# Hybrid Mamba-2 and dilated-attention layer: group 0's B and C beside the samples' values, and one norm matmul a group

## The reference

```python
u = _rmsnorm(x, norm_w) @ w_in                       # 1024 -> z, x|B|C, dt, q, k, v, z_att, gates
xbc = silu(causal_conv(xbc, conv_state, conv_w) + conv_b)
xs, Bm, Cm = split(xbc)                              # B and C: one 128-wide vector per group, 4 groups
dt = softplus(dt_raw + dt_bias);  A = -exp(a_log)
y = ssd_chunked(xs, dt, A, Bm, Cm, ssm_state) + d_skip * xs
yg = (y * silu(z)) per group of 512 channels
yg = yg * rsqrt(mean(yg * yg over the group) + EPS)  # the grouped norm
br_ssd = (yg * ssd_norm_w) @ w_ssd_br
# attention: three head groups, (window, dilation) = (128,1), (512,4), (2048,16)
o = sum over g of alpha_g * o_g,  alpha = softmax of the groups' log sums
br_att = (o * silu(z_att)) @ w_att_br
out = x + (sigmoid(g_ssd) * br_ssd + sigmoid(g_att) * br_att) @ w_out
```

## Time and profile before

| | us |
|---|---|
| median of 3 runs | 1121.01 |
| lowest, highest | 1118.74, 1121.52 |
| the profiled execution's own time | 1128.53 |
| its span | 1126.7 |
| mean granted clock of PE | 0.962 of full speed |
| PE busy | 1032.8 (92% of the span) |
| DVE, ACT, POOL busy | 701.6, 534.6, 242.0 |

### The profile page before, as it was taken

The page is one execution under the profiler, slowest core; times in us unless marked ns, Lnnn a source line. Parts: engine busy times, 40 slices in busy tenths (PEclk is TensorE's granted clock), DMA queues, the critical chain, the costliest instruction groups (busy, mean ns, idle before and its releaser), DMA issues.

```text
span 1126.7 us, 21757 instructions
## 1 busy us (share of the span) xinstructions
PE 1032.8 (92%) x8474; PEld 953.1 (85%) x8474; DVE 701.6 (62%) x1113; ACT 534.6 (47%) x1273; POOL 242.0 (21%) x327
## 2 busy tenths in 40 slices
PE   3999898898989897999999999999998999599998
PEld 2999788888888875359998998998998999599998
DVE  6867574656566357545887887887853576933432
ACT  5335556455555645115546456556443775511210
POOL 0312121222222100001211212112200988300000
PEclk9999999999999998768999999999998999799999
DMA  9543443254511245542533561571496997332221
GB/s 366 225 178 114 156 192 130 83 236 143 232 60 56 83 161 208 161 176 113 229 136 150 230 247 41 227 284 61 173 351 262 338 348 313 121 118 111 75 104 48
DMA packets 30310, 198.28 MB, mean 176 GB/s; under 512 B 4536, under 2 KB 6808, under 8 KB 20704
## 3 DMA queue, kind: packets, MB, share of 16 engines
q1 hardware_dynamic: 25712, 183.35, 42.8%
q0 software_dynamic: 4496, 13.54, 3.1%
HBM read 180.16 MB, written 104.70 MB: 253 GB/s over the span
## 4 chain that ended last, share of the span: by engine, by line
PE 58%; DVE 18%; ACT 13%; issue 7%; DMA 3%; SPq 0%; POOL 0%; DVEq 0%; ACTq 0%; POOLq 0%
PE bank L677 32%; PE bank L711 8%; ACT wH L1259 4%; PE bank L724 4%; DVE cacc L1674 3%; PE bank L900 2%; ACT Sx L1423 1%; DMA slot<-in_state_ssm 1%; DVE wL L1653 1%; PE bank L998 1%; DMA w_raw<-in_weights 1%; PE bank L1016 1%; PE bank L980 1%; PE bank L800 1%; DVE yL L2099 1%
## 5 line engine op out<-in xcount | busy, mean ns | idle before, releaser
L1653 DVE TENSOR_TENSOR wL<-w_raw,wH 128x2048 fp32r<-128x2048 f32 (+1 forms) x63 | 145.6, 2311 | 110.6 <-ACT wH L1259 109.3
L677 PE MATMUL bank<-xH,wH 128*128 128x260 f32 x976 | 205.2, 292 | 6.4 <-DVEq L1598 3.9
L677 PE MATMUL bank<-xH,wL 128*128 128x260 f32 x976 | 197.8, 284 | 0.0
L677 PE MATMUL bank<-xL,wH 128*128 128x260 f32 x976 | 197.5, 284 | 0.0
L677 PEld LDWEIGHTS bank<-xH,wH 128*128 128x128 f32 x976 | 151.4, 190 | 17.4 <-issue 15.2
L1259 ACT CAST wH<-w_raw 128x2048 fp32r<-128x2048 f32 (+1 forms) x63 | 119.0, 1889 | 92.7 <-PE bank L677 83.9
L711 PE MATMUL bank<-wH,xH 128*128 128x256 f32 x480 | 143.6, 299 | 18.3 <-DVEq L1598 11.1
L677 PEld LDWEIGHTS bank<-xL,wH 128*128 128x128 f32 x976 | 151.8, 190 | 0.0
L677 PEld LDWEIGHTS bank<-xH,wL 128*128 128x128 f32 x976 | 151.8, 190 | 0.0
L711 PE MATMUL bank<-wL,xH 128*128 128x256 f32 x480 | 138.2, 288 | 0.0
L711 PE MATMUL bank<-wH,xL 128*128 128x256 f32 x480 | 137.9, 287 | 0.0
(11 more groups left out here) (294 smaller groups left out, 2086.2 us busy)
## 6 DMA issues: line engine op xcount, KB each, us to landing
w_raw<-in_weights SPq DMA_DIRECT2D x62, 1024.0 KB, 5.2
out_kvs<-in_cache SPq DMA_DIRECT2D x16, 2044.0 KB, 10.7
ring<-in_cache SPq DMA_DIRECT2D x48, 256.0 KB, 3.7
slot<-in_state_ssm SPq DMA_DIRECT2D x16, 512.0 KB, 6.5
out_ssm_s<-slot POOLq DMA_DIRECT2D x16, 512.0 KB, 7.0
out_kvs<-in_cache SPq DMA_DIRECT2D x8, 508.0 KB, 6.8
out_kvp<-st POOLq DMA_DIRECT2D x18, 128.0 KB, 3.9
out_kvp<-vv POOLq DMA_DIRECT2D x18, 128.0 KB, 5.2
```

What stands on the lines that cost most here:

```text
L677: mm = pe.matmul(bk[hf].tile[:, 0:HALF], wslot(w, i)[:, k, s * P:(s + 1) * P], x[:, k, hf * HALF:(hf + 1) * HALF], start=(k == 0 and n == ...
L1653: TT(wL[:, i % 2, 0:k * n], raw[:, i % 2, 0:k * n], wH[:, i % 2, 0:k * n].bitcast(F32), ALU.subtract)\
```

## The change

- In `plan()`: `mergeexps` comes at key step 1 instead of 3, and `DT_AT` is 5 instead of 6. The banks of the merge and of the spreads are others.
- All eight tiles of unit B of group 0 stand ahead of `sampleprobs` (six before, the other two at the value stage's end). A new step `convstate` behind them holds SP's load of the convolution's state and DVE's scaling of the taps; both stood later (the load in the middle of the values, the scaling behind the barrier).
- In the value stage the `use` of B stands at value 2, the eight tiles of C at values 1, 3, 6, 8, 11, 13, 16 and 18, and the `use` of C at value 20 (`C_USE`), ahead of the first `valuesum`. Both, and C's whole projection, stood behind the barrier.
- `dtrows` comes right behind `decays`. `dsb` is one matmul of `oddE` and `dsM`, which DVE builds from the identity in `decays` (two reductions, a copy and a product); the load of `sel3` is gone.
- For groups 0 to 2 POOL adds the four squares in three additions of 128x512, and PE makes one matmul with `mean_g` instead of four, in the middle of unit 0 of z, behind four of its eight tiles. What ACT and DVE do for the norm stands there too, behind the `use` of x's unit 1, which it preceded. Group 3 is as before.
- The buffers lie in other places, so that `buf`, `BT`, `CT` and the rest do not overlap what the value stage still reads.

Cut to its core:

```diff
-DT_AT = 6
+C_USE = 20
+DT_AT = 5
...
-        if p == 3:
+        if p == 1:
             out.append(("mergeexps",))
...
-    out += bc_tiles[:KD - 2] + [("sampleprobs", 0), ("sampleprobs", 1), ("selfprobs",), ("dt", 3), ("split", ITEM_AT["x", 0])]
+    out += bc_tiles + [("sampleprobs", 0), ("sampleprobs", 1), ("selfprobs",), ("dt", 3), ("split", ITEM_AT["x", 0]), ("convstate",)]
+    c_tiles, c_use = tiles(("bc", 0), 1)
...
+        if i == 2:
+            out.append(use)
+        if i % 5 in (1, 3) and c_tiles:
+            out.append(c_tiles.pop(0))
+        if i == C_USE:
+            out.append(c_use)
         if i == HALF_DONE + 1:
             out.append(("valuesum", 0))
-    out += bc_tiles[KD - 2:] + [("valuesum", 1), ("gated",), ("barrier",), ("decays",)]
+    out += [("valuesum", 1), ("gated",), ("barrier",), ("decays",), ("dtrows",)]
...
         use = proj("x", 2 * g, unit=0)
         out += [("bc", g), use]
+        if g > 0:
+            out.append(("gsquare", g - 1))
         use = proj("x", 2 * g, unit=1)
         if g > 0:
-            out += [("gsquare", g - 1), ("ssdA", u), ("gnorm", g - 1)]
+            out += [("ssdA", u)]
...
         for kind, j in (("z", 2 * g), ("x", 2 * g + 1), ("z", 2 * g + 1)):
             use = proj(kind, j, unit=0)
+            if g > 0 and u == PER_GROUP * g:
+                _, i, units = out.pop()
+                steps = [("proj", i, units, k) for k in range(KD)]
+                out += steps[:KD // 2] + [("gnorm", g - 1)] + steps[KD // 2:]
...
-            return banks[(0, 1, 4)[i % 3]]
-
-        merge_banks = [banks[i] for i in (2, 6, 0, 3, 7, 1)]
+            return banks[((0, 1, 4) if i < SPREAD_FIRST else (4, 2, 3))[i % 3]]
+
+        merge_banks = [banks[i] for i in (0, 2, 6, 1, 3, 7)]
...
-                    for u in range(UNITS):
-                        mm = pe.matmul(banks[5].tile[:, u * 2 * B:(u + 1) * 2 * B], sel3[:, u, :], dsS[:, :],
-                                       start=True, stop=True)
+                    pe.matmul(banks[5].tile[:, 0:UNITS * 2 * B], oddE[:, :, :].rearrange("p e d -> p (e d)"),
+                              dsM[:, :, :].rearrange("p u b -> p (u b)"), start=True, stop=True).then_inc(banks[5].filled, 1)
...
-                elif op == "valuesum" and a[0] == 0:
+                elif op == "convstate":
                     sp.wait_ge(S["sample_exps"], 2)
...
+                elif op == "gsquare" and a[0] < GROUPS - 1:
+                    g = a[0]
+                    pool.wait_ge(S["y_squared"], 4 * g + 1)
+                    add = nc.gpsimd.tensor_tensor
+                    add(sq2[0][:, :], sq2[0][:, :], sq2[1][:, :], ALU.add).then_inc(S["y_squared"], 1)
+                    add(sq2[2][:, :], sq2[2][:, :], sq2[3][:, :], ALU.add).then_inc(S["y_squared"], 1)
+                    pool.wait_ge(S["y_squared"], 4 * g + 3)
+                    add(sq2[0][:, :], sq2[0][:, :], sq2[2][:, :], ALU.add).then_inc(S["y_squared"], 1)
```

More of the change, by code:

```diff
@@ L220, in plan @@
             use = proj("bc", g, unit=0)
-            out += [("ssdS", u - 1), ("ssdE", u)]
-        out.append(use)
-        use = proj("bc", g, unit=1)
-        out += [("ssdY", u - 1), ("ssdZ", u - 1)] if g > 0 else [("dtrows",)]
-        out.append(use)
+            out += [("ssdS", u - 1), ("ssdE", u), use]
+            use = proj("bc", g, unit=1)
+            out += [("ssdY", u - 1), ("ssdZ", u - 1), use]
         use = proj("x", 2 * g, unit=0)
         out += [("bc", g), use]
+        if g > 0:
+            out.append(("gsquare", g - 1))
         use = proj("x", 2 * g, unit=1)
         if g > 0:
-            out += [("gsquare", g - 1), ("ssdA", u), ("gnorm", g - 1)]
+            out += [("ssdA", u)]
         else:
@@ L454, in hybrid_kernel @@
         lr = a2.tile("lr", [P, 2])
+        VD = nc.alloc_sbuf_tensor_at("VD", [P, 2, T], F32, offset=a2.at)
+        SD = nc.alloc_sbuf_tensor_at("SD", [B, NG, SLOTS, B], F32, offset=a2.at + 4 * T)
+        pself = nc.alloc_sbuf_tensor_at("pself", [P, 2, NG, SLOTS], F32, offset=a2.at + 4 * T + 4 * NG * SLOTS * B)
+        turned_ = a2.at + 12 * T
+        mtmp = nc.alloc_sbuf_tensor_at("mtmp", [P, T], F32, offset=a2.at + 8 * T)
+        KT = a2.tile("KT", [P, 4, HP, NKEYS + 1])
+        selfK = a2.tile("selfK", [P, NG * HP * B])
         gta = a2.tile("gta", [P, R])
@@ L458, in hybrid_kernel @@
         qz = a2.tile("qz", [P, NG, B, HP * SLOTS])
[L459 removed]
+        at = Arena(nc, merge_end_ - 4 * NG * T, merge_end_)
         onesm = at.tile("onesm", [HEADS, R])
@@ L480, in hybrid_kernel @@
         kept_ = a3.at
+        Brm = a3.tile("Brm", [P, NT, P])
+        CBm = a3.tile("CBm", [P, NT, P])
+        yb = a3.tile("yb", [P, T])
+        assert a3.at >= merge_end_ - 4 * NG * T
         tail = a3.tile("tail", [P, XU, TAIL])
@@ L485, in hybrid_kernel @@
         wcv = a3.tile("wcv", [P, XU, TAPS + 1])
-        BT = a3.tile("BT", [P, CONV])
-        CT = a3.tile("CT", [P, CONV])
+        assert a3.at <= merge_end_ + 12 * T
         xu = a3.tile("xu", [P, 3, CONV])
-        Brm = a3.tile("Brm", [P, NT, P])
-        CBm = a3.tile("CBm", [P, NT, P])
         zs = a3.tile("zs", [P, 2, R])
@@ L495, in hybrid_kernel @@
         Lb = a3.tile("Lb", [P, 2, NT, P])
-        dcol = a3.tile("dcol", [P, HEADS, NT])
         hst = a3.tile("hst", [P, 2, NT, P])
@@ L499, in hybrid_kernel @@
         nac = a3.tile("nac", [P, NT, HEADS])
-        yb = a3.tile("yb", [P, T])
+        dcol = a3.tile("dcol", [P, HEADS, NT])
+        assert a3.at <= turned_
+        a3.at = turned_
+        BT = a3.tile("BT", [P, CONV])
+        CT = a3.tile("CT", [P, CONV])
         sq2 = [nc.alloc_sbuf_tensor_at(f"sq2{i}", [P, T], F32, offset=kept_ - 4 * R * (2 - i)) for i in range(2)]
@@ L506, in hybrid_kernel @@
         ad = Arena(nc, base, ceil_)
-        sel3 = ad.tile("sel3", [HEADS, UNITS, P])
+        oddE = ad.tile("oddE", [HEADS, 2, HD])
+        odd = ad.tile("odd", [HEADS, 2])
+        own_pair = ad.tile("own_pair", [HEADS, UNITS])
+        dsM = ad.tile("dsM", [HEADS, UNITS, 2 * B])
         dends = ad.tile("dends", [HEADS, HEADS, NT])
@@ L995, in _ @@
                     banks[7].take(pe, ("gn", g))
-                    pe.wait_ge(S["y_squared"], g + 1)
-                    for k in range(PER_GROUP):
-                        mm = pe.matmul(banks[7].tile[:, :], mean_g[:, :], sq2[k][:, :], start=(k == 0), stop=(k == PER_GROUP - 1))
+                    if g < GROUPS - 1:
+                        pe.wait_ge(S["y_squared"], 4 * g + 4)
+                    else:
+                        pe.wait_ge(S["y_squared"], 4 * g + 1)
+                    n = PER_GROUP if g == GROUPS - 1 else 1
+                    for k in range(n):
+                        mm = pe.matmul(banks[7].tile[:, :], mean_g[:, :], sq2[k][:, :], start=(k == 0), stop=(k == n - 1))
                     mm.then_inc(banks[7].filled, 1)
@@ L1969, in _ @@
                     dve.sem_inc(S["ac_parts_ready"], 1)
+                    heads = con[0:HEADS, C_ID:C_ID + HEADS]
+                    V.tensor_reduce(odd[:, :], heads.rearrange("p (u e) -> p e u", e=2), AX.X, ALU.add)
+                    ch.link(V.tensor_reduce(own_pair[:, :], heads.rearrange("p (u e) -> p u e", e=2), AX.X, ALU.add))
+                    V.tensor_copy(oddE[:, :, :], odd[:, :].unsqueeze(2).to_broadcast([HEADS, 2, HD]))
+                    TT(dsM[:, :, :], dsS[:, :].unsqueeze(1).to_broadcast([HEADS, UNITS, 2 * B]),
+                       own_pair[:, :].unsqueeze(2).to_broadcast([HEADS, UNITS, 2 * B]), ALU.mult).then_inc(S["ac_parts_ready"], 1)
                     TT(dends[:, :, :], con[0:HEADS, C_ID:C_ID + HEADS].unsqueeze(2).to_broadcast([HEADS, HEADS, NT]),
```

32 lines of the change are left out of this document (11 added, 21 removed).

## The result

The changed kernel takes 1134.84 us in the median (1130.41 to 1136.2, 4 runs) against 1121.26 (1118.74 to 1122.13, 4 runs) of the kernel before, measured side by side: the ratio is 1.0098, with a 95% interval of 1.0065 to 1.0132, or 11 us (7 to 15) slower; the medians themselves lie 13.6 apart, inside that interval. The forecast was 1131, slower by 10. The profiled execution has a span of 1134.4 us, 7.7 more than that of before.

A forecast was written before the change was run, and what follows sets the result against it. PE, busy 92% of the span, was taken as the bound, with its clock level deciding the value stage. Front part −7 and norm +17 gave +10 on the median 1121.0: 1131 us, range 1105 to 1146 (8 in 10).

The forecast's parts named there:

- the front part: All up to x: between +7.7 us at half clock and −22.7 at full; −7 taken.
- the norm part: Norm of three groups: 4.0 us of delay and 1.7 of lost clock each, +17 us in all.
- The price of 6.15 for what is late next: Score stage, last za tile to dt 2: table load 1.28, gate .67, wH 1.89, wL 2.31 us.
- all up to the values is 7.0 us earlier: Score stage: dt 2 starts at 430.5 instead of 437.6, moving everything up to the values 7.0 us earlier.
- the middle of the two levels: Value stage: taken between all at half clock, +22.7 us, and all at full clock, −6.1.
- The new wait ahead of the first sum over heads: Value stage: use of C on DVE delays VD; PE waits 4.3 us at half clock, 5.3 at full.
- The two stops: Groups 1 to 3: PE waits about 2.3 us mid z for POOL's additions, then y is 4.0 us late.
- All in a row: Norm: POOL's five operations, DVE's two and the taps run one after another, ending at 614.5; y 4.6 us late.
- The first (exclusion does not bite): Norm: POOL's stages slip between DVE's, clock kept, a group loses 1.3 us; 1118 us in all, chance .20.
- The second (full clock in the value stage): Clock stays full in the value stage and over the short stops; 1110 us, faster, chance .20.
- The third (half throughout, 1146): Value stage: clock stays half throughout, front part +7.7 with norm +17; 1146 us, chance .15.
- the fourth, waits for the spreads' banks: Value stage: spreads wait for banks 2 and 3 until ACT copies B; at most +2 us, no chance given.

The follow-up runs named there:

- score_only: Kernel before with the merge's exps at key step 1, DT_AT 5 and the changed kernel's merge banks: 1118.35 us, ratio 0.9986.
- dsm_only: Kernel before with dsb as one matmul of oddE and dsM, and no load of sel3: 1116.14 us, ratio 0.9949.
- norm_mid4: Changed kernel without POOL's three additions; PE makes four mean_g matmuls mid z, ACT's log stays behind x's convolution: 1126.31 us, ratio 1.003.
- norm_spare: norm_mid4 with POOL's three additions put back, written to a spare tile that nobody reads: 1137.47 us, ratio 1.0131.
- front_c_behind: Changed kernel with before's norm, C's eight tiles in one block behind the values, use of C behind dtrows: 1112.3 us, ratio 0.9899.
- front_c_after: Changed kernel with before's norm, C's eight tiles between decays and dtrows, use of C behind dtrows: 1112.2 us, ratio 0.9907.

## Why the prediction was right

**The total** was right (+10, measured +11, interval 7 to 15), by two errors of opposite sign, so by luck in part: the front part was taken as −7 and gave −1 (−3 to +1.5), the norm part as +17 and cost 13.6 (10 to 17).

**Score stage.** `dt 2` was to start at 430.5 and the first value at 449.7; they stand at 431.2 and 450.3. The price of 6.15 for what is late next was right (6.0, from the last za tile at 425.2). What failed is "all up to the values is 7.0 us earlier" as a gain: score_only, with this part alone, kept 1.6 us (−0.9 to 4.1) of it. Ten profiles of kernels with the new score stage had a wait of 2.6 to 3.7 us ahead of the values, and nine of these had the clock at half for 3 to 16 us of the stage's first half, while in the four with the old stage it was full to 462 or beyond. The prediction had the half level at the stage's start, but set it against a stage of before that was itself at half.

**Value stage.** This is the step that failed most. Its sum started at "before, 456.7 to 497.3 is 40.6 us", a stage that had run at half for 34 us in the profiled execution. The median execution was 7.5 us shorter, and the prediction saw that and added the same +10 to it "since the terms are stretches of work and not of that difference". They were not: a second profile has 31.6 us there. Against 31.6 the changed kernel's 46.1 is 14.5 longer, where I had +8 for the middle of the two levels. The middle itself was about right (46.1 measured, 63.3 and 34.5 the ends), but the base was one draw of two. The price of the full clock was too good as well: "before at full clock would be 22.8" halves the time at half, but the second profile has 31.6 with only 7 us at half, so about 28 at full throughout (an estimate from that profile). A run of values costs .96 us from start to start at full and 1.82 at half, and PE then waits for cached values and longer for `VD`. The new wait ahead of the first sum over heads was sized at 4.3 to 5.3 and was 5.43.

**Behind the barrier.** 4.5 us to x predicted, 5.2 measured, at half clock. DVE's four new operations take .17, .16, .21 and .41 in the trace of after, .95 in all; 1.0 was taken. Against the 12.5 of the first profile that is 7.3 of the gain of 8; dsm_only alone had 5.7 of time.

**The norm.** The two stops, their places and their releasers are as predicted: mid z 2.15 to 2.17 us (2.3 predicted), y 3.2 late (1.3 to 4.6, 4.0 taken), 1.2 of it (1.3 predicted) from the log's place, as norm_mid4 shows, and the other 2.0 from POOL, as norm_spare shows (2.1 there). The term that was too large is the 4.0. "All in a row" had 10.2 us from the end of ACT's squares to the end of the taps; it was 9.0 (597.7 to 606.7 in group 1), because POOL's first addition ran before DVE had an operation of two SBUF operands. The other end, "where POOL's last product comes behind the taps, 3.4", lies nearer only by its number: the last product ended 0.6 us before the last tap. The clock was given 1.7 a group; what is left of the 13.7 beside 3 × 3.2 is 4.1 for three, 1.4 a group: none in group 1, 2.8 in group 2, 1.4 in group 3. From group 1 to 2 and from 2 to 3 it is 84.2 and 87.1 us, where 85 to 87 was said.

**The rivals.** The first (exclusion does not bite) fell; its price of 1.3 is what norm_mid4 measured without POOL. The second (full clock in the value stage) fell for the changed kernel as a whole. The page that has a TensorE kept busy stay at full clock (the Trainium skill, "TensorE: Matmul & The Clock Gate", "Why this matters for your kernels") does not hold in the first profile of before, busy 3.00 of 3.00 us at 0.50; in the second, busy 2.82 to 3.00, the clock was full. The third (half throughout, 1146) fell with the full clock from 463 to 483, and of the fourth, waits for the spreads' banks, the trace of after has none. That C's tiles lift the clock, for which I gave the front part half of its range, is not borne out by the times of front_c_behind and front_c_after.

What stays open is why the same instructions get the full clock in one execution and half in another. The two profiles of before differ from 462 on with the same order and the same waits ahead of it (1.56 and 1.33 us); no run here tells the causes apart. The three like stops of norm_mid4, with the half level behind one of them, say the same within one execution.

## What to carry to other kernels

Work given to an idle engine is not free even when nobody waits for its result: three additions on POOL, 4.6 us of its idle time, cost 3.8 us a group (norm_spare against norm_mid4). They push POOL's two products onto DVE's taps, and the two engines slow each other there: y comes 2.1 us later. The rest fits the clock.

Before a sum is made against a profiled execution, compare its time with the median: 7.5 us between them lay mostly in one stage at the other clock level, and a term whose base is that stage inherits it. Move a step ahead of a wait only after listing what waits behind it in the queue; a single position of one list (`C_USE` 20 or 21) was 6 us. And where runs of one kernel fall into two sets, as those of norm_mid4, one profile shows one set only.
